# Two-layer hybrid decoder trunk: experts and logits chosen in two stages, and the first pair's rows picked with the residual stationary in four parts between gate_up's quarters

## The chip, the cores and the metric

One core of one Trainium2 chip runs the whole program in one launch. The metric is the device time of one execution in microseconds (us); the time before is 1326.63 us, the median of three runs (1325.08 to 1327.33).

## The reference, cut to what matters

512 tokens of 1024 channels, float32, two layers. Layer 0 mixes tokens by sliding-window attention, layer 1 by a gated short convolution. Each is followed by a hierarchical mixture of experts, and at the end by an RMS norm:

```
h = h + mixer(rms_norm(h))
x = rms_norm(h)
g = argmax(softmax(x @ w_group + b_group))            # 1 of 4 groups, probability g_prob
e1, e2 = top2(softmax((x @ w_expert + b_expert)[g]))  # 2 of the group's 8 experts, renormalised
h = h + sum over e in (e1, e2) of
        g_prob * e_prob[e] * ((silu(x @ gate[e]) * (x @ up[e])) @ w_down[e])
```

There are 32 experts of 1024 x 512 (gate), 1024 x 512 (up) and 512 x 1024 (down). In float32 an expert's weights are 6.3 MB and a layer's 201 MB, each read once.

## The kernel before

**Pairs and rounds.** `experts(l)` of each engine walks over 16 pairs of experts (`PAIRS`). Each expert has 64 places (`BLOCK`), so that a pair fills 128 rows. A token's place within its expert is its `rank`. A second round for fuller experts exists under `If(most > BLOCK)`.

**Weights.** A pair's weights are six pieces of 2 MB (`PIECES`), four of gate_up and two of down. They go through a ring of eleven places (`RING`), which lie in buffers that the rest of the layer uses too. SyncE's `load_experts` first issues pieces 0 to 10 (`early`), each as its buffer is given up, and then, in the order of use, piece n as soon as the piece 11 before it has been used. It waits on the counts `gu_done` (gate_up) and `down_done`. The first pair's gate_up pieces hold two channel slices of both experts each ("quarters"), and each is given up by itself. All other gate_up pieces hold four slices of one expert and are given up two at a time, and the two pieces of down, one for each expert, together after the whole of down. So piece 11 waits for the first quarter of pair 0, pieces 12 to 14 for its other quarters, and 15 and 16 for the end of its down.

**Router.** TensorE turns the residual's tiles (`turn_tile`), multiplies each by the router's weights (`logits`, 16 instructions for a tile of 128 tokens), and runs ten 512-wide filler matmuls (`keep_busy(5)`). VectorE's `router(l)` waits for all four tiles' logits, chooses group and experts for all of them in one pass (L1654 to L1684, with `step` a wait for the instruction before), and signals `mask_ready`. TensorE counts ranks by a product with a triangular matrix and three with ones (L1134, L1136) and runs a filler. VectorE computes `rank` (L1693, L1695) and the one-hot `first_sel` (L1696), which says which token stands in which place of pair 0. Then it builds the table of gates and the selection of pair 0 (`select`, L1721).

**First pair.** The other pairs' rows come by an indirect DMA from a copy of the residual and are turned by TensorE (`turn_picked`, L1157). Pair 0's are picked from SBUF by `pick_first` (L1228): selection stationary, residual moving, four tiles added up, in two halves of the channels. ScalarE copies each half (`by_channel`, L832), TensorE turns it (`turn_first`, L1236), and VectorE scales it into `xg` (`take`, L1756). Between the quarters of gate_up (L1184) stand the second half's turn, `index` (L1150; place numbers and gates of a pair, from which the next gather gets its rows), `count` (L1144) and `turn_ranks` (L1164). After gate_up follow silu (L811), the hidden product (L1766), its turn (L1202), the turn of pair 1's rows and down (L1209).

Of the kernel before, what the change touches and what calls it, by code (L numbers as in the profile page):

```python
# [5 lines left out]
P = 128  # L6
# [32 lines left out]
def build_trunk(nc, x, norm_mix, norm_ffn, final_norm, rel_bias, w_qkv, b_qkv, w_o, b_o, sinks,  # L39
# [24 lines left out]
    with ExitStack() as ctx:  # L64
# [129 lines left out]
        by_channel = picked.rearrange("p (q k) -> p q k", k=DT)  # L194
# [118 lines left out]
        EARLY = 3  # L313
        round_ready = [sem(f"round_ready{l}") for l in range(L)]
# [23 lines left out]
        def ups_before(l, i):  # L338

            return l * (2 * PAIRS + 2) + (2 * i + 2 if i else 0)  # L340
# [53 lines left out]
        def logit_bank(l):  # L394

            return ps[0 if l else 4]
# [37 lines left out]
        def _(sp):  # L434
# [27 lines left out]
            def load_experts(l):  # L462
# [57 lines left out]
            for q in range(QUARTERS):  # L520
# [11 lines left out]
                if q < BIG_SLOTS:  # L532
                    sp.wait_ge(main.down_done, 2 * LAST if q == 0 else 2 * PAIRS)
# [22 lines left out]
        def _(pool):  # L556
# [3 lines left out]
            nc.gpsimd.iota(iota[:], [[1, BLOCK]], base=0, channel_multiplier=0,  # L560
                           allow_small_or_imprecise_dtypes=True).then_inc(consts_ready, 1)
            nc.gpsimd.iota(slot_id[:], [[0, 1]], base=0, channel_multiplier=1,
                           allow_small_or_imprecise_dtypes=True).then_inc(consts_ready, 1)
            nc.gpsimd.iota(expert_of[:], [[2, PAIRS]], base=0, channel_multiplier=0,
                           allow_small_or_imprecise_dtypes=True).then_inc(consts_ready, 1)
            nc.gpsimd.iota(base[:], [[0, 1]], base=NONE, channel_multiplier=-1,
# [57 lines left out]
            for l in range(L):  # L624
# [5 lines left out]
                for i in range(PAIRS):  # L630
                    n = l * PAIRS + i
                    if i:
                        gather(S, l, l * LAST + i - 1, i % AHEAD, 2 * n)
# [32 lines left out]
        def _(act):  # L666
# [129 lines left out]
            for t in range(2, TT):  # L796
                root(1, t)
                take_turned(1, t - 1)
# [21 lines left out]
            def take_high(S, n, slot=0):  # L820

                act.wait_ge(S.sums_ready, 2 * n + 2)
                for c in range(2):
                    act.wait_ge(S.down_done, 2 * n + c + 1)
# [3 lines left out]
            def experts(l):  # L828
                S = main
                for half in range(2):  # L830
                    act.wait_ge(early_ps, l * EARLY + half + 1)
                    nc.scalar.activation(by_channel[:, :, 4 * half:4 * half + 4],  # L832
# [597 lines left out]
        def _(dve):  # L1430
# [202 lines left out]
            def router(l):  # L1633
# [23 lines left out]
                for t in range(TT):  # L1657
                    ins = V.max(gm[:, t, :], gp[:, t, :])
# [334 lines left out]
```

## Time and profile before

| | us |
|---|---|
| median of 3 runs | 1326.63 |
| profiled execution's own time | 1326.05 |
| its span | 1324.3 |
| TensorE busy | 1276.9 (96%) |
| VectorE busy | 571.1 (43%) |
| ScalarE busy | 274.6 (21%) |
| DMA | 450.09 MB, mean 340 GB/s |
| chain that ended last | TensorE 79%, DMA 16%, VectorE 3%, ScalarE 1% |

The span is divided into attention (0 to about 180), the experts of layer 0 (188 to 647), the convolution (651 to 838), the experts of layer 1 (854 to 1311) and the last norm. In the page's 40 slices the DMA rate stands at 424 to 429 GB/s in nearly every slice of the two expert stages. The profiled execution's own time is 1.75 us more than its span, and 0.58 us below the median.

### The profile page before, as it was taken

Reading aid. Unit: us, or ns where it says so; the run is one execution under the profiler, and the core shown is the slowest. Engines: PE = TensorE matmul, PEld = TensorE weight load, DVE = VectorE, ACT = ScalarE, POOL = GpSimd, SP = SyncE. Lnnn points to the kernel's source line nnn. Section 1 sums busy time; section 2 is a strip of 40 time slices with the busy share of each in tenths; the row PEclk is TensorE's granted clock in tenths of the full one; section 3 lists DMA queues with packets and bytes.
Section 4 is the critical chain, followed back from the end, with each engine's and each line's share of the span. In section 5 each row is a group of like instructions: output and inputs, shape, how many; then the busy total and the mean of one; then the engine's idle time right before and its main releaser. Section 6 shows DMA issues by size and latency. Waiting matters only on the chain.

```text
span 1324.3 us, 14801 instructions
## 1 busy us (share of the span) xinstructions
PE 1276.9 (96%) x6002; PEld 682.8 (52%) x6002; DVE 571.1 (43%) x1262; ACT 274.6 (21%) x561; POOL 108.7 (8%) x119
## 2 busy tenths in 40 slices
PE   7999999999999999999999999999999999989996
PEld 5777663444444443444578888634444444434443
DVE  5586342443343433333575662424343343433334
ACT  4257611011101110000452221110111001110003
POOL 3950000000000000000000000000000000000000
PEclk8999989999999999999999999899999999999998
DMA  9301978999999999999632339779999999999994
GB/s 345 106 1 39 423 301 351 429 425 427 426 426 426 427 424 428 427 427 427 174 122 85 105 139 392 299 310 427 428 426 426 427 428 426 427 425 427 427 427 161
DMA packets 66187, 450.09 MB, mean 340 GB/s; under 512 B 17608, under 2 KB 32994, under 8 KB 40516
## 3 DMA queue, kind: packets, MB, share of 16 engines
q1 hardware_dynamic: 60144, 436.09, 79.6%
q0 software_dynamic: 5472, 11.95, 2.3%
q8 instruction: 50, 0.82, 0.3%
q10 hardware_dynamic: 500, 1.06, 0.2%
q14 instruction: 21, 0.17, 0.0%
HBM read 450.74 MB, written 6.32 MB: 345 GB/s over the span
## 4 chain that ended last, share of the span: by engine, by line
PE 79%; DMA 16%; DVE 3%; ACT 1%; issue 0%; SPq 0%; DVEq 0%; ACTq 0%
PE ps L1184 26%; PE ps L971 20%; PE ps L1209 14%; PE ps L1176 7%; DMA big<-in_moe_w_gate_up_dram 6%; DMA arena<-in_moe_w_gate_up_dram 6%; DMA small<-in_moe_w_gate_up_dram 3%; PE ps L1157 2%; PE ps L1113 1%; PE ps L929 1%; PE ps L1228 1%; PE ps L1202 1%; PE ps L1052 1%; PE ps L1019 1%; PE ps L1170 1%; PE ps L1150 1%
## 5 line engine op out<-in xcount | busy, mean ns | idle before, releaser
L1184 PE MATMUL ps<-big,arena 128*64 128x512 f32 x784 | 299.3, 603 | 4.6 <-DMA small<-in_moe_w_gate_up_dram 3.5
L1184 PE MATMUL ps<-arena 128*64 128x512 f32 x528 | 208.7, 594 | 1.9 <-DMA big<-in_moe_w_gate_up_dram 1.9
L1184 PE MATMUL ps<-small,arena 128*64 128x512 f32 x368 | 163.6, 608 | 4.4 <-DMA big<-in_moe_w_gate_up_dram 3.8
L1822 DVE TENSOR_TENSOR h<-ps,h 128x512 f32<-128x512 f32 x240 | 149.1, 684 | 11.2 <-PE ps L1176 11.2
L1184 PEld LDWEIGHTS ps<-big,arena 128*64 128x64 f32 x784 | 91.1, 139 | 118.3 <-issue 118.3
L1176 PE MATMUL ps<-arena_parts 128*128 128x512 f32 x512 | 135.1, 406 | 1.7 <-DVE arena_parts L1781 1.7
L1209 PE MATMUL ps<-big,arena 128*64 128x512 f32 x336 | 134.5, 595 | 0.0
L811 ACT ACTIVATE gain<-ps,slot_root 128x512 f32<-128x512 f32 x32 | 37.0, 1157 | 445.8 <-PE ps L1184 445.8
L1209 PE MATMUL ps<-arena 128*64 128x512 f32 x320 | 127.5, 595 | 0.0
L1781 DVE SCALAR_TENSOR_TENSOR arena_parts<-ps,slot_gate,arena_parts 128x512 fp32r<-128x512 f32 x64 | 48.0, 751 | 172.6 <-ACT arena_parts L825 172.6
L1176 PEld LDWEIGHTS ps<-arena_parts 128*128 128x128 f32 x512 | 91.2, 188 | 52.4 <-issue 35.0
L1775 DVE TENSOR_SCALAR arena_parts<-ps,single 128x512 fp32r<-128x512 f32 x32 | 24.0, 751 | 212.9 <-PE ps L1170 212.9
L971 PE MATMUL ps<-xt_parts,small_parts 128*128 128x512 f32 x288 | 111.3, 395 | 3.0 <-DVE xr_parts L1465 1.9
L971 PE MATMUL ps<-xr_parts,small_parts 128*128 128x512 f32 x272 | 106.5, 392 | 0.0
L1766 DVE SCALAR_TENSOR_TENSOR gain<-ps,slot_root,gain 128x256 f32<-128x256 f32 x64 | 38.0, 673 | 158.7 <-PE ps L1184 152.8
L971 PE MATMUL ps<-xt_parts,big_parts 128*128 128x512 f32 x256 | 100.3, 392 | 0.0
L1184 PEld LDWEIGHTS ps<-arena 128*64 128x64 f32 x528 | 63.1, 136 | 69.8 <-issue 69.8
L825 ACT ACTIVATE arena_parts<-ps,slot_gate 128x512 fp32r<-128x512 f32 x64 | 44.0, 687 | 209.8 <-PE ps L1209 209.8
L1184 PE MATMUL ps<-xr,arena 128*64 128x512 f32 x192 | 82.9, 603 | 2.5 <-DMA xt<-in_moe_w_gate_up_dram 2.3
L1184 PE MATMUL ps<-xt,arena 128*64 128x512 f32 x176 | 81.0, 615 | 2.2 <-DMA big<-in_moe_w_gate_up_dram 2.2
L1184 PEld LDWEIGHTS ps<-small,arena 128*64 128x64 f32 x368 | 49.2, 140 | 57.0 <-issue 57.0
L1209 PE MATMUL ps<-small,arena 128*64 128x512 f32 x176 | 77.9, 595 | 0.6 <-ACT arena L816 0.6
(219 smaller groups left out, 1660.8 us busy)
## 6 DMA issues: line engine op xcount, KB each, us to landing
big<-in_moe_w_gate_up_dram SPq DMA_DIRECT2D x49, 2048.0 KB, 28.6
arena<-in_moe_w_gate_up_dram SPq DMA_DIRECT2D x33, 2048.0 KB, 28.9
small<-in_moe_w_gate_up_dram SPq DMA_DIRECT2D x23, 2048.0 KB, 25.7
big<-in_moe_w_down_dram SPq DMA_DIRECT2D x21, 2048.0 KB, 28.4
arena<-in_moe_w_down_dram SPq DMA_DIRECT2D x20, 2048.0 KB, 32.2
xr<-in_moe_w_gate_up_dram SPq DMA_DIRECT2D x12, 2048.0 KB, 29.2
small<-in_moe_w_down_dram SPq DMA_DIRECT2D x11, 2048.0 KB, 32.1
xt<-in_moe_w_gate_up_dram SPq DMA_DIRECT2D x11, 2048.0 KB, 26.5
```

What stands on the lines that cost most here:

```text
L811: nc.scalar.activation(hid, ps[2][:].rearrange("q (p k) -> q p k", p=P), ACT.Silu, scale=slot_root[:, slot:slot + 1]).then_inc(S.silu_read ...
L825: nc.scalar.activation(parts(y_high[:, c, :]), ps[6 + c][:], ACT.Copy, scale=slot_gate[:, slot:slot + 1]).then_inc(S.high_ready, 1)
L929: nc.tensor.matmul(ps[bank][:], ident[:], ident[:].unsqueeze(1).to_broadcast([P, 4, P]), start=True, stop=True)
L971: mm = nc.tensor.matmul(bank, parts(a), parts(b), start=start and a is left and b is right, stop=stop and a is left_low)
L1157: mm = nc.tensor.transpose(ps[bank + d // 4][:, (d % 4) * P:(d % 4 + 1) * P], picked.rearrange("p (q k) -> p k q", k=DT)[:, d, :], ident[:])
L1176: mm = nc.tensor.matmul(ps[bank + n][:], parts(selT[:, slot, t * P:(t + 1) * P]), parts(y[:, c, :]), start=y is y_high, stop=y is y_low)
L1184: mm = nc.tensor.matmul(ps[2 + half][j * BLOCK:(j + 1) * BLOCK, :], xg[:, k, j * BLOCK:(j + 1) * BLOCK], ws[j][:, k % per, half * FF:(half ...
L1209: mm = nc.tensor.matmul(ps[6 + c][j * BLOCK:(j + 1) * BLOCK, :], hidT[:, k, j * BLOCK:(j + 1) * BLOCK], ws[j][:, k, c * HALF:(c + 1) * HAL ...
L1766: V.scalar_tensor_tensor(out=hid[:, :, ks], in0=ps[3][:].rearrange("q (p k) -> q p k", p=P)[:, :, ks], scalar=slot_root[:, slot:slot + 1], ...
L1775: V.tensor_scalar(parts(selT[:, slot, :]), ps[4][:], slot_id[:, 0:1], None, ALU.is_equal)\
L1781: V.scalar_tensor_tensor(out=parts(y_low[:, c, :]), in0=ps[6 + c][:], scalar=slot_gate[:, slot:slot + 1], in1=parts(y_high[:, c, :]), op0= ...
L1822: ins = V.tensor_tensor(hs, ps[bank + c][:], hs, ALU.add)
```

## The change

The logits of tile 2 are computed before tile 3 is turned, and tile 3's go to another bank. VectorE chooses for tiles 0 to 2 as soon as they are there, then for tile 3. The groups that were not chosen get a large negative number instead of being summed away, so that the second search finds the expert's number directly. Ranks, places and experts count from 1. `first_sel` is built before the gates' table. The ten fillers (and in layer 1 two more) go; two are put between the rank products of the two stages.

`pick_first(q)` has the residual's channels stationary (every eighth, so a stride of 8 elements) and `first_sel` moving: the result has channels on partitions, as gate_up wants it, with no copy and no turn. It has four parts of two channel slices. Parts 0 and 1 stand ahead of gate_up, part 2 after its first quarter and part 3 after its second. `turn_ranks` and `count` move behind gate_up, the first `spread` behind down, `find_slots` of pair 0 into pair 1's turn. The pieces of pairs 0 and 1 (`SPLIT`) all hold a quarter of gate_up or half of down for both experts, and each is given up when it has been used. In the convolution one `split_low_of` of VectorE moves from the end of its first turn to the front of it.

```diff
+        SPLIT = 2
+        SELECTS = PAIRS + 1
+        LATE = TT - 1
+        FIRST_BANKS = (0, 1, 4, 6)
...
-                    if c < 4 and i == 0:
-                        w = w_gate_up[l, 0:2].rearrange("e (p k) n -> p e k n", p=P)[:, :, 2 * c:2 * c + 2]
-                        sp.dma_start(both_experts(ring[l][n]), w).then_inc(ring_in[n], 16)
+                    if i < SPLIT:
+                        w, c = (w_gate_up, c) if c < 4 else (w_down, c - 4)
+                        sp.dma_start(both_experts(ring[l][n % RING]), w[l, 2 * i:2 * i + 2].rearrange(
+                            "e (p k) n -> p e k n", p=P)[:, :, 2 * c:2 * c + 2]).then_inc(ring_in[n % RING], 16)
...
                     if used < 4:
-                        sp.wait_ge(main.gu_done, ups_before(l, before) + (used // 2 if before else used) + 1)
+                        sp.wait_ge(main.gu_done, ups_before(l, before) + (used if before < SPLIT else used // 2) + 1)
                     else:
-                        sp.wait_ge(main.down_done, 2 * (l * PAIRS + before + 1))
+                        sp.wait_ge(main.down_done, downs_before(l, before) + 1 if before < SPLIT and used == 4
+                                   else downs_before(l, before + 1))
...
+            logits(0, 2)
             turn_tile(1, 3)
-            logits(0, 2)
             logits(0, 3)
-            keep_busy(5)
...
-                nc.tensor.matmul(ranks[:, 0:TT], upper[:], marks, start=True, stop=False)
+                nc.tensor.matmul(ranks[:, 0:1], upper[:], marks[:, 0:1], start=True, stop=True)
+                for t in range(LATE):
+                    nc.tensor.matmul(ranks[:, t + 1:TT], ones,
+                                     marks[:, t:t + 1, :].to_broadcast([P, TT - 1 - t, E]),
+                                     start=(t == 0), stop=False)
+                nc.tensor.matmul(ranks[:, 1:LATE], upper[:], marks[:, 1:LATE], start=False, stop=False)
+                keep_busy(1, 7)
+                pe.wait_ge(mask_ready, 2 * l + 2)
+                nc.tensor.matmul(ranks[:, LATE:TT], upper[:], marks[:, LATE:TT], start=False, stop=True).then_inc(rank_ps, 1)
                 keep_busy(1, 6)
...
+                def pick_first(q, tiles=range(TT)):
+                    for d in (2 * q, 2 * q + 1):
+                        for t in tiles:
+                            mm = nc.tensor.matmul(ps[FIRST_BANKS[q]][:, d % 2 * P:(d % 2 + 1) * P],
+                                                  h[:, t].rearrange("p (q k) -> p k q", k=DT)[:, d, :],
+                                                  first_sel[:, t].rearrange("p j s -> p (j s)"),
+                                                  start=(t == 0), stop=(t == TT - 1))
+                    mm.then_inc(first_done[q % 2], 1)
...
+                    if i == 0:
+                        pe.wait_ge(early_taken, l * EARLY + 1)
+                        gate_up(both((0, 1)), part(i, 0), 2).then_inc(S.gu_done, 1)
+                        pick_first(2)
+                        pe.wait_ge(S.rows_taken, 2 * n + 1)
+                        gate_up(both((2, 3)), part(i, 1), 2).then_inc(S.gu_done, 1)
+                        pick_first(3)
+                        pe.wait_ge(S.selected, l * SELECTS + 3)
+                        index(S)
+                        pe.wait_ge(early_taken, l * EARLY + 2)
...
+            def down_split(S, n, first, second):
+                ws = first()
+                pe.wait_ge(S.hidT_ready, 2 * n + 1)
+                down_steps([(0, 0), (1, 0)], ws, 2)
+                pe.wait_ge(S.hidT_ready, 2 * n + 2)
+                down_steps([(0, 1), (1, 1)], ws, 2).then_inc(S.down_done, 1)
+                ws = second()
+                down_steps([(2, 0), (3, 0)], ws, 2).then_inc(S.down_done, 1)
+                down_steps([(2, 1), (3, 1)], ws, 2).then_inc(S.down_done, 1)
...
+                dve.wait_ge(logits_ps, TT * l + LATE)
+                choose(slice(0, LATE))
                 dve.wait_ge(logits_ps, TT * (l + 1))
...
+                choose(slice(LATE, TT))
...
-                step(V.tensor_scalar(rank[:], rank[:], -1.0, None, ALU.add))
```

## Rows read from the trace of the kernel before

**Rows 1.** Head of the page: the span.
```profile
span 1324.3 us, 14801 instructions
```
**Rows 2.** Chain that ended last, end of layer 0's experts: start us, us, what.
```profile
584.31 41.37 DMA big<-in_moe_w_gate_up_dram
...
635.95 7.09 PE ps L1209 x32
```
**Rows 3.** Windows, after the busy times: TensorE's clock, DMA share, GB/s.
```profile
193.00:194.00 1.00, 1.00 0.80 344
...
195.00:200.00 5.00, 1.00 0.00 0
...
201.00:202.00 1.00, 1.00 1.54 279
...
226.00:256.00 30.00, 30.00 (x145) 12.62 (x142) 10.68 (x21) 3.19 (x5) 1.29 (x2) 1.00 1.00 426
...
792.00:800.00 8.00, 1.00 1.01 428
...
859.00:860.00 1.00, 1.00 0.99 426
```
**Rows 4.** Timeline of SyncE's queue: issue of pieces 11 and 15, both layers.
```profile
200.16 0.33 SPq L479 DMA_DIRECT2D arena<-in_moe_w_down_dram  x1
...
223.93 0.33 SPq L479 DMA_DIRECT2D arena<-in_moe_w_gate_up_dram  x1
...
865.59 0.33 SPq L479 DMA_DIRECT2D arena<-in_moe_w_down_dram  x1
...
889.35 0.33 SPq L479 DMA_DIRECT2D big<-in_moe_w_gate_up_dram  x1
```
**Rows 5.** Chain that ended last, layer 0's router and first two pairs.
```profile
171.44 1.71 PE ps L1113 x16
...
196.53 3.59 PE ps L1184 x16
...
201.10 0.92 PE ps L1144 x8
...
216.87 7.02 PE ps L1209 x32
...
244.02 7.02 PE ps L1209 x32
```
**Rows 6.** Timeline of TensorE, end of pair 0's gate_up, turn of pair 1.
```profile
209.83 3.65 PE L1184 MATMUL ps<-small,arena 128*64 128x512 f32 x16
...
215.81 1.05 PE L1157 MATMUL ps<-ident,arena 128*128 128x128 f32 x8
```
**Rows 7.** Groups by line, TensorE's weight loads: busy us, mean ns.
```profile
L1157 PEld LDWEIGHTS ps<-ident,arena 128*128 128x128 f32 x240 | 29.1, 191 | 0.0
```
**Rows 8.** Timeline of VectorE in the two routers.
```profile
174.09 0.69 DVE L1470 COPY xt<-ps 128x512 f32<-128x512 f32 x1 [1.92 <-PE ps L946]
...
179.77 0.33 DVE L1654 TENSOR_TENSOR arena<-ps,rstd 128x160 f32<-128x160 f32 x1 [4.32 <-PE ps L1113]
...
180.49 0.37 DVE L1658 MAX8 arena<-arena 128x8 f32<-128x8 f32 x4
...
184.89 0.29 DVE L1684 TENSOR_TENSOR arena<-arena 128x128 f32<-128x128 f32 x1
...
187.76 0.69 DVE L1696 TENSOR_TENSOR arena<-iota,rank 128x512 f32<-128x512 f32 x1
...
839.48 0.69 DVE L1470 COPY xt<-ps 128x512 f32<-128x512 f32 x1 [1.26 <-PE ps L946]
...
853.18 0.69 DVE L1696 TENSOR_TENSOR arena<-iota,rank 128x512 f32<-128x512 f32 x1
```
**Rows 9.** Windows of layer 0's router: busy PE, PEld, DVE, ACT, POOL, then clock.
```profile
178.00:184.00 6.00, 6.00 (x15) 3.42 (x15) 3.88 (x33) 0.27 (x2) 0.00 (x0) 0.50 1.04 444
184.00:185.00 1.00, 1.00 (x4) 0.52 (x3) 0.90 (x5) 0.16 (x1) 0.00 (x0) 0.96 0.81 344
```

More of the change, by code:

```diff
@@ L1251, in weights, with part @@
                     return [ring[l][(i * PIECES + c + j) % RING] for j in range(2)]
[L1253 to L1255 removed]
+                def part(i, c):
+                    ring_loaded(pe, l, i, c)
+                    place = both_experts(ring[l][(i * PIECES + c) % RING])
                     return [place[:, j] for j in range(2)]
@@ L1262, in experts @@
                     n = o + i
-                    pe.wait_ge(S.rows_taken, 2 * n + 1)
-                    if i:
+                    if i == 0:
+                        pe.wait_ge(early_taken, l * EARLY + 1)
[7 more added lines that the diff above has]
+                        pe.wait_ge(early_taken, l * EARLY + 2)
+                    elif i < SPLIT:
+                        pe.wait_ge(S.rows_taken, 2 * n + 2)
+                        for c in range(2):
+                            gate_up(both((2 * c, 2 * c + 1)), part(i, c), 2).then_inc(S.gu_done, 1)
+                    else:
                         pe.wait_ge(S.rows_taken, 2 * n + 2)
@@ L1267, in experts @@
                         gate_up(both((0, 1, 2, 3)), ws).then_inc(S.gu_done, 1)
-                    else:
-                        gate_up(both((0, 1)), quarter(0), 2).then_inc(S.gu_done, 1)
-                        turn_first(1, 4)
-                        pe.wait_ge(S.selected, o + l + 3)
-                        index(S)
-                        count(l)
-                        turn_ranks()
-                        gate_up(both((2, 3)), quarter(1), 2).then_inc(S.gu_done, 1)
                     if i:
+                        pe.wait_ge(S.selT_ready, n)
                         spread(S, n, i)
                         pe.wait_ge(S.y_ready, 2 * n)
-                        pe.wait_ge(S.selT_ready, n)
+                        if i == 1:
+                            pe.wait_ge(route_ready, l + 1)
                         pe.wait_ge(S.added, l * ADDS + TT * (i - 1))
@@ L1282, in experts @@
                         add_tile(i - 1, 1, 6)
-                    if i:
+                    if i < SPLIT:
+                        gate_up(both((4, 5)), part(i, 2), 2).then_inc(S.gu_done, 1)
+                        if i == 0:
+                            pe.wait_ge(S.rows_taken, 2 * n + 2)
+                        last_quarter(S, part(i, 3), 2)
+                    else:
                         ws = weights(i, 2)
@@ L1286, in experts @@
                         last_quarter(S, ws)
-                    else:
-                        pe.wait_ge(S.rows_taken, 2 * n + 2)
-                        gate_up(both((4, 5)), quarter(2), 2).then_inc(S.gu_done, 1)
-                        pe.wait_ge(early_taken, (l + 1) * EARLY)
-                        spread(S, n, i)
-                        last_quarter(S, quarter(3), 2)
                     if i:
@@ L1297, in experts @@
                     if i + 2 < PAIRS:
-                        pe.wait_ge(S.selected, n + l + 4)
+                        pe.wait_ge(S.selected, l * SELECTS + i + 4)
                         index(S)
-                    pe.wait_ge(S.selT_ready, n + 1)
+                    if i:
+                        pe.wait_ge(S.selT_ready, n + 1)
+                    else:
+                        turn_ranks()
+                        count(l)
                     turn_hidden(S, n)
```

214 lines of the change are left out of this document (106 added, 108 removed).

## The prediction

> **What bounds the kernel now.** I read the 40 slices first, then the chain, then the DMA windows, then SyncE's queue, and last TensorE and VectorE between the logits and the first down.
>
> TensorE is busy 96% of the span, yet it doesn't set the end of an expert stage. A pair costs it 27.15 us (downs start at 216.87 and 244.02 [rows 5]). Fifteen more pairs after the first down (223.89) would end at 631.1. The last down of layer 0 ends at 643.04 [rows 2], 11.9 us later, since gate_up waited for weights up to 584.31 + 41.37 = 625.68 [rows 2]. The DMA moves 426 GB/s from 226 on [rows 3]: a 2.097 MB piece takes 4.92 us, and six pieces and a gather of 64 rows of 4 KB (an estimate, 0.6 us) make 30.1 us for a pair. So the end of a layer's experts is the time at which the weights flow without a gap, plus a fixed time.
>
> They don't flow at once. In layer 0 the eleven early pieces are in at 193.8; from 195 to 200 nothing moves [rows 3]. Piece 11 is issued at 200.16 [rows 4], when the first quarter of gate_up has ended (196.53 + 3.59 [rows 5]), and data flows about 1.3 us later, from 201.3 [rows 3]. Four pieces (19.7 us, 0.6 for a gather) end near 221.6, but piece 15 waits for down and is issued at 223.93 [rows 4]. From there until 625.68 the queue is never empty: 79 pieces in 400.5 us, 5.07 each. Layer 1 does the same: early pieces in at 860.0 [rows 3], piece 11 at 865.59, piece 15 at 889.35 [rows 4]. Whatever brings **the issue of piece 15** forward brings the layer's end forward by as much, down to a floor: the early pieces' end, plus 20.3 us for four pieces and a gather, less 1.3. That is 212.8 in layer 0 (11.1 us to win) and 879.0 in layer 1 (10.35 us).
>
> **Up to the selection.** In layer 0 logits of tile 2 (1.71 us [rows 5]) now come before tile 3's turn, so the turn starts at 174.7, and VectorE's copy, at 174.09 before [rows 8], starts at 175.65. The copy, a reciprocal and three table operations take 1.4 us, and the choice for three tiles starts at 177.05 instead of 179.77 [rows 8]. One pass over four tiles took 179.77 to 185.18 [rows 8], 5.41 us. Of it some 0.66 is for each tile (MAX8 0.09, from 0.37 for four [rows 8], once for groups and once for experts; match and find about 0.14, twice; six wide operations at 0.04 each for 32 to 40 elements, from 0.33 for 160 and 0.29 for 128 [rows 8]), so 2.77 is fixed. A pass of the new form leaves out a reduction, the index correction and two subtractions (about 1.0, at 0.2 to 0.4 each) and adds 0.07 per tile and some waiting: 1.8 to 2.0 fixed. Three tiles then take 4.05 and one 2.6, together 6.7. Bounds: 5.4 (no more than before) and 9.4 (all that the earlier start wins is lost). The mask is done at 183.75.
>
> TensorE meanwhile has ten fillers less. The clock was 1.2 GHz (0.50) from 178 to 184, after the narrow logits, and back at 2.4 GHz (0.96 of the window) in 184 to 185, while fillers ran [rows 9]. I take the low clock for the new rank products (0.96 us) and two fillers (1.7): from the first mask at 181.1 they end at 183.8, as the second mask comes. One product and the semaphores take 0.5. VectorE's rank takes 0.33 (the second pass over it, 0.26, goes) and first_sel 0.69 [rows 8]. It ends at 185.4 instead of 188.45: 3.05 us earlier. Layer 1: the copy moves from 839.48 [rows 8] to 839.99 (two fillers go, one set of logits comes ahead), the choice starts 1.4 us after it at 841.4, the same 8.3 us follow (177.05 to 185.4): 849.7 against 853.87 [rows 8], 4.15 us. The gates' table is now built after first_sel (about 2.3 us with select, done 2.3 us after it), beside 3.5 us of picking; without that cover it would cost its 2.3.
>
> **From the selection to piece 15.** The price of a pick is not in the trace: 16 instructions of 128 columns, each with its own 128 x 128 float32 weights, strided by 8 elements. The nearest row is the turn of pair 1: eight of 128 columns with the same stride of 8 on the stationary side, 1.05 us in all, so 0.11 each [rows 6]. Sixteen two-pass float32 products with their own weights took 1.71 us in the logits [rows 5]. Both say 1.75 us for a part. Upper bound: a load (0.191 [rows 7]) that is not hidden, plus 0.11, so 4.8 us; lower bound 1.71.
>
> The Trainium skill ("TensorE: Matmul & The Clock Gate", The mechanism) says that a weight load overlaps with a running matmul only where the row group differs. Here every load fills all rows, so by that rule each part would take the 4.8 us. The eight turns with loads of 0.191 us in 1.05 us contradict it, and the measurement decides. What the rule would give stands among the rivals.
>
> So TensorE, from first_sel on: two parts 3.5, index 0.34, first quarter 3.6 [rows 5], semaphores 0.1 = 7.5, and piece 11 is issued at 192.9 and 857.2 instead of 200.16 and 865.59. Then part 2 (1.75), a quarter (3.5, half of 7.02), part 3 (1.75), index 0.34, two quarters 7.0 = 14.3. From the end of gate_up to down it was 213.48 [rows 6] to 216.87 [rows 5] = 3.4 us, of which about 1.65 is waiting for silu and the hidden product. Index, turn_ranks (four turns, 0.44) and count (0.92 [rows 5]) make 1.7 and now fill it: 3.45. Then the first half of down, 3.5, gives up the place of piece 15. Sum 28.8 us; before it was 188.45 to 223.93, 35.5. VectorE's four takes (about 0.45 each) lie beside index and picks. Piece 15: 185.4 + 28.8 = 214.2 (9.7 us earlier) and 849.7 + 28.8 = 878.5 (10.85, of which the floor allows 10.35).
>
> **Does the flow then hold?** With piece 15 flowing at 215.5, piece 23 could start at 255.7 and is given up at about 252.9 (first half of pair 2's gate_up); piece 27 could start at 275.8, given up near 273.2. With 1.3 us to the first data there are about 1.3 us to spare, and more with each pair. TensorE ends pair 0 at 218.1, 5.8 us earlier, so its margin at the layer's end is 11.9 - (9.7 - 5.8) = 8.0 us: the DMA still ends last. Pieces of 8 KB runs instead of 16 cost nothing: layer 1's first four, which have them, moved at 428 GB/s [rows 3]. The convolution's split_low_of: VectorE has the same work before TensorE's third block either way, which waits for its end in both orders: 0, between -0.5 and +0.5. Everything behind a layer's experts hangs on their end and moves with it.
>
> Sum: 9.7 + 10.35 = 20.05. I take off 1.0 for small waits, a clock that is back a little later, and TensorE's clock dips in the last pairs: 19.0. The profiled execution's own time is the span of 1324.3 [rows 1] and 1.75 around it, 1326.05; that becomes 1307.0, and on the median, 0.6 higher, 1307.6.
>
> **Rivals.**
> - *The clock comes back late* (17%). It was low for the whole router [rows 9], and now TensorE idles about 2.5 us where fillers ran. If it stays at 1.2 GHz through the last filler and parts 0 and 1, these cost 3.5 + 0.4 more in each layer, 7.3 in all with the floor: 1314.9. Against it: from the first mask on TensorE has nearly gapless work.
> - *The choice gains nothing* (11%): two passes with their waits take 9.4 us, or something holds the first one. Then only the 6.7 us behind the selection are won, twice: 1313.2.
> - *The loads of the picks are not hidden* (4%), the slower side. Four parts at 4.8 instead of 1.75 add 12.2 us: piece 15 comes 2.5 us later than before in layer 0 and 1.35 later in layer 1: 1330.5. It decides from 4.3 us for a part (20.55 / 8 over 1.75), 0.27 us per instruction.
> - *The restart doesn't set the end* (3%): something else, a later starvation or TensorE, and the time stays at 1326.6. Against it stands the 426 GB/s in every window.
>
> **How the numbers follow.** The forecast has 65%, on its own 1305 to 1310. Its best is the floor of both layers, 21.45: 1305.2. The two middle rivals reach to 1315, a mixture of both to 1317. I give 1305 to 1316. A median of this kernel can tell about 0.2%, 2.6 us, from no change. Faster by more 93%, same 3%, slower 4%.
>
> **What would show it.** Right: piece 11 issued near 193 and 857, piece 15 near 214 and 878.5; the gap in the DMA's rate from 194 to 201 shrunk to 1 us or so; a pick of 16 instructions in 1.75 us; two choices of about 4 and 2.6 us; 79 pieces of 5.07 behind piece 15. Wrong: a clock of 0.5 in the windows of parts 0 and 1, picks above 2 us, or DMA windows below 420 GB/s between 230 and 300.

## The result, and the profile after

| us | before | after |
|---|---|---|
| median | 1325.66 (1324.59 to 1327.33, 6 runs) | 1331.05 (1327.89 to 1332.83, 6 runs) |
| profiled execution's own time | 1326.05 | 1327.89 |

The ratio is 1.0035, with a 95% interval of 1.0025 to 1.0044. The change makes the kernel slower by 0.35%; 1307.6 had been forecast, and the range ended at 1316. Between the two profiled executions the difference is 1.84 us.

The page's first line answers to [rows 1]:

```profile
span 1326.1 us, 14953 instructions
```

SyncE's queue in the kernel after (start us, us, what) answers to [rows 4]. These are pieces 11 and 15 of layer 0 and then of layer 1:

```profile
199.15 0.37 SPq L480 DMA_DIRECT2D arena<-in_moe_w_down_dram  x1
...
225.07 0.33 SPq L487 DMA_DIRECT2D arena<-in_moe_w_gate_up_dram  x1
...
864.28 0.37 SPq L480 DMA_DIRECT2D arena<-in_moe_w_down_dram  x1
...
890.21 0.33 SPq L487 DMA_DIRECT2D big<-in_moe_w_gate_up_dram  x1
```

Piece 11 comes 1.0 and 1.3 us earlier than before, but piece 15 comes 1.14 and 0.86 us later. The forecast had 214.2 and 878.5. The chain at the end of layer 0 (compare [rows 2]) shows that piece 15 still carries the end:

```profile
587.84 39.98 DMA big<-in_moe_w_gate_up_dram
...
638.09 7.09 PE ps L1218 x32
```

Down ends at 645.18, 420.11 us after the issue of piece 15; before it was 419.11. So the lateness is not made behind piece 15. The chain of layer 0 from the rank products to the first down (start us, us, what; compare [rows 5]) shows where it is made:

```profile
181.61 0.64 PE ps L1140 x2
...
184.01 1.81 PE ps L936 x2
185.82 0.27 PE ps L1148 x2
...
187.57 7.61 PE ps L1250 x32
...
195.52 3.60 PE ps L1193 x16
199.11 4.00 PE ps L1250 x16
203.11 3.58 PE ps L1193 x16
206.70 4.00 PE ps L1250 x16
...
211.04 7.02 PE ps L1193 x32
...
221.44 7.02 PE ps L1218 x32
```

L1250 is the pick. A part of 16 instructions takes 4.00 us, not 1.75, and parts 0 and 1 together take 7.61. They start at 187.57 and not at 187.24, when `first_sel` is there, since a second pair of fillers (L936, 186.09 to 187.57) still holds TensorE. The quarters of gate_up between them (3.60, 3.58) have the length that the forecast gave them. The line's own view (ns min/median/max, first and last start us) says what a pick consists of:

```profile
L1250 PEld LDWEIGHTS ps<-arena,h x64: 313/335/339, 187.3 to 210.2; 128*128 128x128 f32 x64
L1250 PE MATMUL ps<-arena,h x64: 398/402/505, 187.4 to 210.3; 128*128 128x128 f32 x64
```

A load of its weights takes 335 ns where the turn's took 191 [rows 7]. Loads follow each other every 0.250 us (4.00 / 16), and so do the products: TensorE waits for its own weights.

The selection too is later than forecast. VectorE (start us, us, operation, and in brackets its idle time before it) answers to [rows 8]:

```profile
177.07 0.27 DVE L1683 TENSOR_TENSOR arena<-ps,rstd 128x120 f32<-128x120 f32 x1
...
181.47 0.19 DVE L1683 TENSOR_TENSOR arena<-ps,rstd 128x40 f32<-128x40 f32 x1
...
184.34 0.16 DVE L1716 TENSOR_TENSOR arena<-arena 128x4 f32<-128x4 f32 x1
186.23 0.29 DVE L1720 SCALAR_TENSOR_TENSOR rank<-ps,arena 128x128 f32<-128x128 f32 x1 [1.72 <-PE ps L1148]
186.55 0.69 DVE L1722 TENSOR_TENSOR arena<-iota,rank 128x512 f32<-128x512 f32 x1
```

The choices take 4.5 us (to 181.57) and 2.8 us. The rank then waits 1.72 us for a product (L1148) that stands behind two fillers (L936). `first_sel` ends at 187.24 instead of 185.4. The windows (us, then busy times, TensorE's clock, DMA share, GB/s) answer to [rows 3] and [rows 9]:

```profile
180.00:185.00 5.00, 3.39 (x12) 2.87 (x13) 4.01 (x27) 0.32 (x2) 0.00 (x0) 0.52 1.02 429
185.00:190.00 5.00, 5.00 (x16) 3.57 (x16) 2.83 (x12) 0.00 (x0) 0.28 (x1) 0.80 1.01 426
...
195.00:200.00 5.00, 5.00 (x25) 2.46 (x25) 1.58 (x6) 0.00 (x0) 0.00 (x0) 1.00 0.00 0
...
206.00:207.00 1.00, 1.00 (x6) 0.38 (x2) 0.00 (x0) 0.00 (x0) 0.00 (x0) 1.00 0.02 8
...
230.00:260.00 30.00, 30.00 (x145) 12.58 (x143) 11.57 (x24) 3.20 (x5) 2.32 (x3) 1.00 1.01 426
```

The gap from 195 to 200 is as long as before. New gaps near 206 and 213 have come, because the first three quarters end 7.6 and 7.9 us apart (SyncE issues at 199.15, 206.74 and 214.67) and a piece takes 4.92 us. From 230 on the flow is whole at 426 GB/s.

### The profile page after: what moved, and what is told of

Read it like the earlier page. It is cut to its first block, busy times and chain, and to the rows that moved or that the text cites. A ratio compares the mean times of both kernels' runs of the same rounds, so it can differ in the third digit from the quotient of the medians.

```text
span 1326.1 us, 14953 instructions
## 1 busy us (share of the span) xinstructions
PE 1276.4 (96%) x6072; PEld 701.4 (53%) x6072; DVE 574.1 (43%) x1282; ACT 272.1 (21%) x557; POOL 108.7 (8%) x119
## 4 chain that ended last, share of the span: by engine, by line
PE 82%; DMA 13%; DVE 4%; ACT 0%; issue 0%; SPq 0%; DVEq 0%
PE ps L1193 29%; PE ps L978 20%; PE ps L1218 14%; DMA big<-in_moe_w_gate_up_dram 9%; PE ps L1185 8%; DMA arena<-in_moe_w_gate_up_dram 3%; PE ps L1250 2%; PE ps L1166 2%; PE ps L1211 1%; PE ps L1059 1%; PE ps L1026 1%; PE ps L1179 1%; PE ps L1120 1%; PE ps L1159 1%; PE ps L1046 1%; PE ps L936 1%
## 5 line engine op out<-in xcount | busy, mean ns | idle before, releaser
L1193 PE MATMUL ps<-big,arena 128*64 128x512 f32 x784 | 293.3, 602 | 8.8 <-DMA small<-in_moe_w_gate_up_dram 3.4
L1193 PE MATMUL ps<-arena 128*64 128x512 f32 x528 | 206.9, 598 | 3.3 <-DMA big<-in_moe_w_gate_up_dram 2.6
L1193 PE MATMUL ps<-small,arena 128*64 128x512 f32 x368 | 152.1, 595 | 1.0 <-DMA arena<-in_moe_w_gate_up_dram 0.7
L1218 PE MATMUL ps<-big,arena 128*64 128x512 f32 x336 | 127.6, 596 | 0.0
L1218 PE MATMUL ps<-arena 128*64 128x512 f32 x320 | 113.6, 595 | 0.0
L1193 PE MATMUL ps<-xr,arena 128*64 128x512 f32 x192 | 77.9, 595 | 0.3 <-DMA xt<-in_moe_w_gate_up_dram 0.3
L1218 PE MATMUL ps<-small,arena 128*64 128x512 f32 x176 | 74.4, 596 | 0.6 <-ACT arena L826 0.6
L1193 PE MATMUL ps<-xt,arena 128*64 128x512 f32 x176 | 74.2, 594 | 0.5 <-DMA big<-in_moe_w_gate_up_dram 0.5
L1193 PEld LDWEIGHTS ps<-small,arena 128*64 128x64 f32 x368 | 46.0, 137 | 46.7 <-issue 46.7
```

The costliest lines, as they stand in the source:

```text
L1193: mm = nc.tensor.matmul(ps[2 + half][j * BLOCK:(j + 1) * BLOCK, :], xg[:, k, j * BLOCK:(j + 1) * BLOCK], ws[j][:, k % per, half * FF:(half ...
L1218: mm = nc.tensor.matmul(ps[6 + c][j * BLOCK:(j + 1) * BLOCK, :], hidT[:, k, j * BLOCK:(j + 1) * BLOCK], ws[j][:, k % per, c * HALF:(c + 1) ...
```

## The experiments

In what follows, "selection to piece 15" is the time from the end of `first_sel` to the issue of piece 15. It is 35.47 us in layer 0 and 35.48 in layer 1 before, 37.83 and 38.04 after. The end of the layer's last down stands behind the issue of piece 15 by 419.1 to 422.8 us in every trace of every kernel here. The stage ahead of `first_sel` is measured from the last but one of the eleven early issues (172.31 in layer 0 and 838.94 in layer 1 after); the last of them leaves 4.6 to 9 us later. Where a time is that of one execution only, the text says so.

**1. The kernel after, unaltered.**

> The changed kernel once more, unaltered, for a second trace and a time beside the other runs. Both theories: 1328 to 1333 us, about 1.004 of the kernel before. Its executions spread over 5 us where those of before spread over 3. Theory 'the clock decides the spread': in a slower execution the granted clock of 1.2 GHz lasts longer after the router than in the fastest one, whose trace has it until about 187 and 852.7. Rival 'the DMA restarts decide it': clock as in that trace, but pieces 12 to 15 issued later.

1331.05, ratio 1.0047 (1.0030 to 1.0064). In its trace (span 1329.0) the selection to piece 15 takes 38.05 and 38.07 us. The low clock lasts from 176.3 to 189.9, 13.6 us where it was 6.8 (180.2 to 187.0) in the first trace. That is the theory of the clock in part only: of the 2.9 us between the two spans, 1.4 have come before the last but one early issue of layer 0, which a low clock in the router can't cause, and 0.7 between it and the end of `first_sel`. The slowdown is there again, and so is its place.

**2. The picks read contiguous channels.**

```diff
-  h[:, t].rearrange("p (q k) -> p k q", k=DT)[:, d, :],
+  h[:, t, d * P:(d + 1) * P],
```

Pair 0's gate_up is loaded with its rows in the matching order (`"(k p) n -> p k n"`, two transfers for a piece), and `take` uses the gains in that order. The same picks are made, with the same count of instructions.

> The picks read 128 adjacent channels as the stationary operand instead of every eighth; so that the products stay right, pair 0's gate_up weights are loaded with the same order of channels and the gain in that order (gcol). Theory 'the stride of the stationary operand is the price': loads fall from 335 ns to about 190, an instruction from 250 to about 107 ns, a part of 16 from 4.0 to 1.75 us, the four parts win 9 us in each layer, piece 15 is issued near 216 (it was 225.1) and 881 (890.2), the time is 1310 to 1314 us. Rival 'a full-row weight load is never hidden behind a running matmul, whatever the layout' (the rule of the Trainium skill that the prediction weighed): a part stays near 4 us, or at 3 (0.19 + 0.107 minus what overlaps, times 16), and the time stays within 1320 to 1332.

1317.44 (4 runs), ratio 0.9946 (0.9927 to 0.9964): 13.6 us less than the kernel after on the same chip. First the view of the pick's line in the window of part 2, then the chain with parts 0 and 1 together and part 2:

```profile
L1256 PE MATMUL ps<-arena,h x16: 275/275/377, 197.3 to 199.0; 128*128 128x128 f32 x16
L1256 PEld LDWEIGHTS ps<-arena,h x15: 189/192/192, 197.4 to 198.9; 128*128 128x128 f32 x15
```

```profile
189.69 3.71 PE ps L1256 x32
...
197.33 1.98 PE ps L1256 x16
```

The load falls from 335 to 192 ns, the part from 4.00 to 1.98 us. Fifteen loads start within 1.5 us, so every 0.107 us: loads that fill all rows of the array do run beside the products. Selection to piece 15 takes 30.28 and 30.34. What made a pick dear is the stride of 8 elements, not the load as such.

**3. The same pair of kernels again, in five rounds.**

> The changed kernel beside the contiguous one on one chip. Both theories: 1.0035 to 1.0045 of the kernel before, 1330 to 1331 us.

> The contiguous picks again, in more rounds, beside the changed kernel. Theory 'the picks' stride is worth 7.5 us in each layer' (38.0 to 30.3 us from first_sel to piece 15 in the traces): 14 to 15 us faster than the changed kernel, 0.993 to 0.995 of before. Rival 'part of it is given back at the end of a layer by the stretches at 1.2 GHz in the last pairs': 9 to 12 us.

The kernel after: 1331.49, ratio 1.0041 (1.0027 to 1.0054). The contiguous one: 1316.47 (1315.36 to 1317.85), ratio 0.9933 (0.9919 to 0.9946). The stride is worth 15.0 us. In the traces, selection to piece 15 falls from 38.08 to 29.93 in layer 0 and from 38.08 to 30.27 in layer 1, together 16.0.

**4. Twice the columns.**

```diff
-  first_sel[:, t].rearrange("p j s -> p (j s)"),
+  first_sel[:, t].rearrange("p j s -> p (j s)").unsqueeze(1).to_broadcast([P, 2, P]),
```

> Each pick streams its 128 selection columns twice (256 columns, the second copy unused), with the strided stationary operand as in the changed kernel. Theory 'the load sets the pace and the stream hides behind it': an instruction stays near 250 ns (256 columns take 213 ns), a part at 4.0 to 4.2 us, the time within 1 us of the changed kernel's per layer. Rival 'load and stream one after the other': 250 + 107 = 357 ns, a part at 5.7 us, 6.8 us more in each layer, 13 us in all, near 1344.

The pick's line in the kernel with 256 columns, and its part 2 in the chain:

```profile
L1250 PEld LDWEIGHTS ps<-arena,h x64: 313/338/339, 188.7 to 211.9; 128*128 128x128 f32 x64
L1250 PE MATMUL ps<-arena,h x64: 402/403/611, 188.8 to 212.2; 128*128 128x256 f32 x64
```

```profile
200.70 4.14 PE ps L1250 x16
```

Its time was 1333.12 in one execution. Double the stream adds 0.14 us to a part. The strided load sets the pace and the stream lies beside it. If loads and streams stood one behind the other, the added 128 columns would have shown in full: by the 0.107 us of a contiguous product that is some 1.7 us for 16 (an estimate).

**5. Four strides in one kernel.** Part q reads channels with a stride of 2, 4, 1 and 8 elements.

```diff
-  h[:, t].rearrange("p (q k) -> p k q", k=DT)[:, d, :],
+  h[:, t, 0:P * (2, 4, 1, 8)[q]:(2, 4, 1, 8)[q]],
```

> The changed kernel whose four parts read the stationary operand with strides of 2, 4, 1 and 8 elements (the products are then not the reference's). Theory 'the stride sets the price of a load, step by step': loads of about 190 ns at stride 1, more at 2 and 4, 335 at 8. Rival 'any stride other than 1 costs the full price': 335 at 2, 4 and 8. Both: piece 15 about 2.3 us earlier or more, since one part is contiguous: 1318 to 1328 us.

The loads in four windows of this kernel, at full clock but for the first few at a stride of 2: stride 1, 8, 2 and 4 in that order. The channels that strides 1, 2 and 4 read are not those that the layer needs, so that this kernel is good for its times only.

```profile
L1250 PEld LDWEIGHTS ps<-arena,h x16: 186/192/192, 200.0 to 201.7; 128*128 128x128 f32 x16
...
L1250 PEld LDWEIGHTS ps<-arena,h x15: 334/334/336, 205.8 to 209.1; 128*128 128x128 f32 x15
...
L1250 PEld LDWEIGHTS ps<-arena,h x12: 196/196/282, 853.5 to 854.8; 128*128 128x128 f32 x12
...
L1250 PEld LDWEIGHTS ps<-arena,h x9: 330/330/330, 855.3 to 857.2; 128*128 128x128 f32 x9
```

In layer 1 parts 0 and 1 (strides 2 and 4) took 5.85 us together, part 2 1.98 and part 3 4.00; the time was 1326.25 in one execution. For a product the price is a step: 192 and 196 ns for strides of 1 and 2, 330 and 334 for 4 and 8. It neither grows in proportion to the stride nor sets in at the first gap. Why the step lies between 2 and 4 elements is not shown here.

**6. Turns in place of products.** With the cause of the wrong price found but not why the turns of [rows 6] are cheap at the same stride, parts 1 and 3 became turns of the residual (`nc.tensor.transpose`), part 1 with a stride of 2 and part 3 with a stride of 8. Parts 0 and 2 stayed products at a stride of 8. As in 5, only the times count.

```diff
+  if q in (1, 3):
+      for t in tiles:
+          mm = nc.tensor.transpose(ps[FIRST_BANKS[q]][:, d % 2 * P:(d % 2 + 1) * P],
+                                   h[:, t].rearrange("p (q k) -> p k q", k=DT)[:, d, :] if q == 3
+                                   else h[:, t, 0:2 * P:2], ident[:])
+      continue
```

> The changed kernel, with parts 1 and 3 replaced by turns (8 instructions each, the residual as stationary operand and the identity moving) at strides of 2 and 8; their products are not the reference's. The prediction took the price of a pick from turns of another buffer. Theory 'the kind of product makes the difference': turns of the residual at stride 8 load in 191 ns and follow each other every 111 ns, as those of the gathered rows do, so part 3 takes 0.9 us, while parts 0 and 2, products at stride 8, stay at 4.0. Rival 'the buffer makes it': loads of 334 ns, 250 ns apart, a part of 2.0 us.

TensorE's timeline in this kernel: part 2, a product, and part 3, the turns, from the same buffer with the same stride. Below it the views of the turns of part 3 and of part 1.

```profile
198.23 4.07 PE L1256 MATMUL ps<-arena,h 128*128 128x128 f32 x16
...
205.81 1.15 PE L1251 MATMUL ps<-ident,h 128*128 128x128 f32 x8
```

```profile
L1251 PEld LDWEIGHTS ps<-ident,h x8: 186/190/206, 205.8 to 206.6; 128*128 128x128 f32 x8
...
L1251 PEld LDWEIGHTS ps<-ident,h x8: 199/209/306, 193.0 to 194.0; 128*128 128x128 f32 x8
```

Its time was 1321.65 in one execution. A turn's strided load takes 190 ns, a product's 334. For the turns the buffer doesn't matter, since the gathered rows gave 191, and at the same buffer and stride the kind of instruction does. The trace shows one difference of kind: a call of a float32 product is two instructions (a part has 8 calls and x16), a turn is one (x8). Whether that makes the price is not shown. For turns the step also lies elsewhere: at a stride of 2 they took 209 ns in part 1 (and in layer 1), against 140 contiguous. So the row on which the forecast leaned was a true measurement of another instruction.

**7. No fillers between the rank products**, in the kernel after.

```diff
-  keep_busy(1, 7)
   pe.wait_ge(mask_ready, 2 * l + 2)
```

> The two fillers between the rank products of the two stages are left out. Theory 'they are on the path': the second mask is there at 184.3, but TensorE is in the fillers at 1.2 GHz until 185.8; without them the rank follows 1.5 us earlier in each layer, 3 us in all: 1325 to 1329. Rival 'the clock needs them': 1.2 GHz lasts some us longer, which takes the gain back: 0 or up to 3 us slower than the changed kernel.

1329.90, ratio 1.0042 (1.0025 to 1.0059), against 1331.05 and 1.0047 for the kernel after on the same chip. Its chain, and the clock while the first picks ran:

```profile
184.53 0.63 PE ps L1147 x2
185.16 1.87 PE ps L936 x2
187.03 7.46 PE ps L1249 x32
```

```profile
187.00:190.00 3.00, 3.00 (x15) 3.00 (x14) 1.27 (x6) 0.00 (x0) 0.00 (x0) 0.50 1.00 423
```

`first_sel` ends at 186.32, 0.9 us earlier, but the picks now wait for the next filler, which ends at 187.03. From the last but one early issue to piece 15 it is 51.95 and 50.25 us in the two layers, where the four traces of the kernel after have 52.8 to 53.7 and 51.3: some 1 us is won in each layer and not 1.5. That is too little for the runs to show. The low clock does last longer (to 190.5), but it costs the strided picks nothing: 32 of them take 7.46 us with 3.5 of it at 1.2 GHz, and 7.46 to 7.61 at full clock in the four traces of the kernel after.

**8. Fillers earlier, and none at all.** Both start from the contiguous kernel. In both the two removals are made; only the first has the two additions, one for each layer.

```diff
   logits(0, 3)
+  keep_busy(2)
...
   logits(1, TT - 1)
+  keep_busy(2)
...
-  keep_busy(1, 7)
...
-  keep_busy(1, 6)
```

> The kernel with contiguous picks, and the fillers placed otherwise: four (two calls) right behind the last logits, where TensorE waited about 3 us for the first mask; none between the rank products and none behind them. Theory 'the low clock and the fillers behind the masks cost the rest of the forecast': the four end at or before the first mask, the clock is back 1 to 3 us earlier, the rank products and the picks start earlier, and piece 15 comes 2 to 3 us earlier in each layer: 1312 to 1314.5 us where the contiguous one took 1317.4. Rival 'the clock comes back when it does, whatever runs': the filler that went (1.5 us of path in the middle) is all that is won, 1315 to 1317.

> The same with no fillers at all from the logits to the picks. Theory 'low clock': the clock stays at 1.2 GHz longer, through the first picks and perhaps into gate_up, so that the time is 1 to 4 us above the one with the four early fillers. Rival 'the clock doesn't matter here, since the loads of the picks set their pace at either level': within 1 us of it.

1317.99 (8 runs), ratio 0.9943 (0.9927 to 0.9959), and 1319.92 (4 runs), ratio 0.9944 (0.9924 to 0.9964). The chain of the first and of the second, with the 32 picks of parts 0 and 1, and then a window of the second:

```profile
187.79 5.47 PE ps L1255 x32
```

```profile
190.80 5.96 PE ps L1254 x32
```

```profile
190.00:194.00 4.00, 3.20 (x15) 3.20 (x16) 2.56 (x12) 0.00 (x0) 0.01 (x1) 0.50 1.01 428
```

In the first the selection takes 13.65 us in layer 0 from the last but one early issue, where it took 15.5 in the contiguous kernel, but the picks fall into the 1.2 GHz stretch and take 5.47 instead of 3.71. What is won ahead of the selection is paid behind it, and the 3 to 5 us that had been forecast did not come. From the last but one early issue to piece 15, both layers together, it is 89.3 us in both traces of the contiguous kernel, 89.5 with the early fillers and 91.4 with none. Where the fillers stand makes no difference here. Going without costs 2 us by one trace and by the medians, and nothing by the ratios, whose intervals reach 2.6 us either way: that stays open.

**9. One choice for all four tiles.** The first kernel of 8, with one pass over all tiles that waits for all logits, which again share a bank.

```diff
-  dve.wait_ge(logits_ps, TT * l + LATE)
-  choose(slice(0, LATE))
   dve.wait_ge(logits_ps, TT * (l + 1))
...
-  choose(slice(LATE, TT))
+  choose(slice(0, TT))
```

> As with the four early fillers, but one pass of the new choice over all four tiles, once all logits are there, and all rank products behind its one mask. Theory 'the two stages win what the prediction says', 1 to 1.5 us in each layer over one pass that starts after the last logits: here 2 to 3 us slower than the staged one. Rival 'a second pass costs as much as its earlier start wins' (one pass of the new form is about 4.8 us from 178.4, the mask at 183.2 against 184.3 for the second stage, but 0.8 to 1.4 us more of rank products behind it): within 1 us of it.

1322.66 (10 runs), ratio 0.9969 (0.9958 to 0.9979); with staging it was 0.9943 on the same chip, so staging is worth about 0.26%, 3.4 us, with intervals that just touch. VectorE's timeline, the one choice and its rank:

```profile
182.53 0.33 DVE L1688 TENSOR_TENSOR arena<-ps,rstd 128x160 f32<-128x160 f32 x1 [3.11 <-PE ps L1126]
...
189.55 0.29 DVE L1723 SCALAR_TENSOR_TENSOR rank<-ps,arena 128x128 f32<-128x128 f32 x1 [1.55 <-PE ps L1153]
```

From the last but one early issue to the end of `first_sel` it is 16.75 us in layer 0 here and 13.65 with two stages, in layer 1 13.48 and 12.41. The choice of one pass also starts behind all logits in one bank, so that what is measured is the staging as a whole.

**10. Piece 15 waits for the whole of down.** From the contiguous kernel:

```diff
-  sp.wait_ge(main.down_done, downs_before(l, before) + 1 if before < SPLIT and used == 4
-             else downs_before(l, before + 1))
+  sp.wait_ge(main.down_done, downs_before(l, before + 1))
```

> The kernel with contiguous picks, but piece 15 (and 21) waits for the whole of down, as 16 does: nothing else changes. Theory 'the issue of piece 15 carries the end of each layer one to one': it comes 3.4 us later in both layers (near 222.7 and 881.4), the DMA is empty for that time, and the time is 6.5 to 7 us above the contiguous kernel, 1324 to 1325 us. Rival 'something else ends the layer': 0 to 2 us above it.

1323.01 (10 runs), ratio 0.9968 (0.9953 to 0.9982). In SyncE's queue pieces 15 and 16 leave together at the end of down:

```profile
225.11 0.33 SPq L493 DMA_DIRECT2D arena<-in_moe_w_gate_up_dram  x1
225.48 0.43 SPq L493 DMA_DIRECT2D big<-in_moe_w_down_dram  x1
```

Selection to piece 15 takes 33.19 and 33.56 instead of 30.28 and 30.34, 6.1 us more over both layers. The last down stands 421.22 and 421.56 us behind it, so the ends moved with it. The medians of this and of the contiguous kernel are 5.6 us apart, but on two chips; by the ratios it is 0.22% or 0.35%, 2.9 or 4.6 us, against the first or the second set of runs of the contiguous kernel, with about 3 us either way. The traces carry this verdict, and the size by runs is smaller than the 6.5 to 7 expected. Giving up a place after half of down is worth 3 us in each layer up to the issue.

**11. Three more executions of the two kernels.**

> The kernel before, unaltered, for a second trace: the two traces of before and after differ by 1.8 us while their medians differ by 5.4. Theory 'the first trace of after was a lucky one': this one is within 1.5 us of 1326, its 1.2 GHz stretch in each router is near 6.7 us, and first_sel ends 16.5 to 17 us after the last attention weights' release (piece 5 issued at 171.5, first_sel at 187.8 to 188.5). Rival 'the first trace of before was a slow one': 1323 to 1325 with first_sel earlier.

> The same once more, with the same two theories: how much the stretch at 1.2 GHz varies from one execution of before to the next.

> The changed kernel once more: how much its stretches at 1.2 GHz vary. Theory 'lucky first trace': 1329 to 1333, with 10 to 13 us at 1.2 GHz in a router against 6.5 in the first trace of after. Rival: 1328, as there.

1325.38, 1326.95 and 1329.41. They correct the picture of before, and none of the theories as it stood. From the last but one early issue to the end of `first_sel` layer 0 took 16.13 us in the trace on which the forecast rests, and 14.49 in both of these; their low clock lasts 3.4 us (179.6 to 183.0 and 179.2 to 182.6), not 6.8 (177.3 to 184.0). The one of after took 1329.41 with 6.8 us at 1.2 GHz, as in the first trace. The mean times over all traces of the two kernels (3 of before, 4 of after), stage by stage:

| stage, us | before | after | difference |
|---|---|---|---|
| start to the last but one early issue, layer 0 | 172.89 | 172.95 | +0.06 |
| to the end of first_sel | 15.04 | 15.29 | +0.25 |
| to piece 15 | 35.47 | 37.97 | +2.50 |
| to the end of the last down | 420.23 | 419.91 | -0.32 |
| to the end of first_sel, layer 1 (with the convolution) | 209.77 | 206.98 | -2.79 |
| to piece 15 | 35.48 | 38.06 | +2.58 |
| to the end of the last down | 419.65 | 420.89 | +1.24 |
| behind the last down | 15.82 | 15.84 | +0.02 |
| span | 1324.33 | 1327.88 | +3.54 |

## Why the prediction was wrong

**The step that failed is the price of a pick**: "Both say 1.75 us for a part." It measured 4.00, and 3.8 in the first two parts. Four parts cost 15.6 us in layer 0 instead of 7.0, and in both layers selection to piece 15 took 37.8 to 38.1 us where 28.8 had been summed. In the first trace that is 9.0 us in layer 0 and 9.2 in layer 1, 18.3 together. 8.6 of the 9.0 are the picks, and 0.33 is a wait that the sum had at nothing: the filler behind the last rank product ends that much after `first_sel` (0.7 in layer 1). The contiguous kernel shows the price by undoing only this (and ordering pair 0's weights to match): 30.3 us and, in the second set of runs, 15.0 us less time.

The upper bound in the text, 4.8 for a load of 0.191 that is not hidden, did cover the 4.00, but by a wrong reason and so by luck, and the range of the time left it out. The Trainium skill ("TensorE: Matmul & The Clock Gate", The mechanism) lets a weight load overlap only where the row group differs. The contiguous loads fill all rows, take 0.192 us and start every 0.107 us beside the products, so the rule is wrong for this kernel, as the forecast said. The load itself was the unknown. It was taken as 0.191 from a turn, and is 0.334 for a product with the same stride. The rival "the loads of the picks are not hidden" had been given 4%, with 4.3 us as the point from which the change loses. Its size nearly came; its mechanism did not: the products still run beside the loads (experiment 4), and it is the loads, longer than assumed, that set the pace.

The trace of before had a warning that was not read: among turns the load depends on the stride. The residual's turns read contiguously and took 140 ns; those of pair 1, with a stride of 8, took 191 [rows 7]. The logits' products, which I set beside the picks, read contiguously. (The forecast calls them two-pass: 8 calls for a tile are 16 instructions in the trace.) Their views in the kernel before:

```profile
L946 PEld LDWEIGHTS ps<-ident,h x32: 138/140/226, 160.6 to 173.7; 128*128 128x128 f32 x32
```

```profile
L1113 PEld LDWEIGHTS ps<-wr,xt x64: 186/192/333, 165.8 to 179.3; 128*128 128x128 f32 x64
```

So there was a row for the turn at both strides and for the product at one. The fourth corner, product and stride of 8, was in no row, and I filled it with the turn's price. From the ratio of the turns (191 / 140) it would have been some 0.26 us (an estimate), and the honest upper bound of the load higher than 0.191.

**Up to the selection**: 185.4 forecast, 187.24 measured in layer 0. In layer 1 it is 13.23 us from the last but one early issue (838.94) to the end of `first_sel`, where the forecast had 11.33 (838.37 to 849.7). So 1.84 and 1.9 us were lost. The choices took 4.5 and 2.8 us instead of 4.05 and 2.6 (the 0.66 for a tile in the forecast is 0.70 by its own parts). The rank products of the first stage took 2.4 us (181.61 to 184.01) instead of 0.96 at the low clock. And so the two fillers, 1.81, ended 1.5 us after the second mask instead of with it. The clock was at 1.2 GHz until 187.0 here, before the first pick, and until 189.9 in another trace. The rival of the late clock was partly right, yet what it cost lay ahead of the picks and not in them. Here they ran at full clock, and where they didn't (experiment 7) the strided ones lost nothing by it.

**The size of the router's gain** was read from one execution of before. In layer 1 the staged router gains 2.25 to 2.3 us in every trace; in layer 0 it gains 0.5 to 1.2 against the trace of the forecast and loses 0.4 to 1.2 against the two others. Experiment 9 speaks for staging, with intervals that just touch.

**What held.** The issue of piece 15 carries each layer's end: 419.1 to 422.8 us in 17 traces whose issue varied by more than 8 us in layer 0. The flow behind it is whole at 426 GB/s. Pieces of 8 KB runs cost nothing (427 GB/s from 792 to 800 after, 428 before), the gates' table is hidden beside the picks, and index, `turn_ranks` and `count` fill the wait for silu: gate_up's end to down took 3.38 us (218.06 to 221.44) of the 3.45 summed. The quarters took 3.6 and 7.02. The choice started at 177.07, where 177.05 had been summed. The move in the convolution is worth nothing, as forecast: from layer 0's last down to layer 1's last but one early issue it is 193.75 us in the other two traces of before and 193.7 to 193.8 in the four of after.

**The sum, mended**, for the two profiled executions. Raw it was 20.55 (9.7 and 10.85). Less 18.3 from selection to piece 15, less 3.7 for the selections, less 1.9 for the flow behind piece 15 (420.11 and 420.03 instead of 419.11 twice), plus 1.6 for the convolution, where only the trace of before has a stretch of low clock (0.72 in the first row below, 1.00 in the second), makes -1.75, that is 1.75 us slower; 1.84 was measured. The medians differ by 5.4 and the means of all traces by 3.54 in span. The profiled execution of after was the fastest of its six, which explains part of it. The other 1.9 us are not settled: runs without a trace can't be divided, and 1.24 of the 3.54 itself lies behind piece 15 of layer 1, where single traces vary by 2.6.

The convolution's first windows in the kernel before, and then in the kernel after. That the low clock makes the whole 1.6 is argued from their coming together (the other two traces of before have a clock of 1.00 in this window and a stage 1.6 us shorter):

```profile
650.00:656.00 6.00, 5.05 (x15) 4.02 (x16) 4.87 (x9) 1.34 (x3) 0.00 (x0) 0.72 0.16 3
```

```profile
650.00:656.00 6.00, 4.11 (x24) 3.35 (x23) 5.46 (x10) 3.47 (x7) 0.00 (x0) 1.00 0.01 3
```

**A better version** came out of it: with contiguous channels the change makes the kernel 0.5 to 0.7% faster than before. In its second trace the span of 1314.7 is 9.4 us above the 1305.25 of the forecast: 3.9 for two later selections, 2.6 for 29.93 and 30.27 where 28.8 was summed, 4.4 for the flow (421.14 and 421.47 instead of 419.11), less the 1.55 that the forecast had taken off for the floor and small waits.

The permutation in the weights' DMA has a price of its own. Pair 0's gate_up comes in runs of 4 KB and in two transfers for a piece, and in layer 1 it moved at 407 GB/s, where the kernel after moved 427 in the same window:

```profile
792.00:800.00 8.00, 8.00 (x37) 6.64 (x36) 1.94 (x2) 0.00 (x0) 0.00 (x0) 1.00 1.02 407
```

It cost no time, since the queue still ran dry behind the early pieces: 0 GB/s from 196 to 198 in layer 0, and 246 and 221 for the two microseconds from 856 in layer 1.

## What to carry to other kernels

A duration is the price of one kind of instruction with one access pattern. Before it is carried to a new instruction, list what differs (kind, stride, passes, clock) and take the unknown corner as unknown on the load, not only on whether the load is hidden. When channels go on partitions by way of the stationary side, read them contiguously and put the permutation into the weights' DMA. Here the slower transfers that this gave were hidden; what they cost where the weights' flow has no gap was not tested. And read a stage's gain from several executions: one router took 16.1 us in one and 14.5 in two others.

## What the runs showed of the hardware

- A float32 128 x 128 stationary load for a product takes 192 ns at a stride of 1 element, 196 at 2, 330 at 4 and 334 at 8 (experiment 5). Loads follow each other every 0.107 us at stride 1 and every 0.250 at 8. For a turn it is 140 ns contiguous, 209 at a stride of 2 and 190 at 8; at 8 they follow each other every 0.11 us.
- Loads that fill all rows run beside the products in both cases: contiguous ones take 192 ns and start every 107, and 256 columns instead of 128 add 0.14 us to 16 strided picks.
- 1.2 GHz makes contiguous picks dearer and strided ones not: 32 take 5.47 us with 3.4 of it at the low clock, against 3.71 with nearly none, and the strided ones 7.46 with 3.5 of it at the low clock, against 7.46 to 7.61 with none.
- Pieces of 2 MB moved at 427 GB/s with runs of 8 KB, and at 407 with runs of 4 KB in two transfers each. Runs and transfers were not varied apart.
- The clock of 1.2 GHz in layer 0's router lasted 3.4 us in two executions of the kernel before and 6.8 in a third; in the kernel after, 6.8 in two and 13.6 in two. Fillers moved it about, and no difference in time beyond the intervals came with that.
